# Attention: VectorE scales unit i-1's probabilities ahead of unit i's mask and maximum

## The reference

```python
def causal_block_attention(q, k, v, scale):
    outs = []
    for blk in range(S // Q_BLOCK):                 # 8 blocks of 128 queries
        q0 = blk * Q_BLOCK
        kend = q0 + Q_BLOCK
        s = jnp.einsum('bqhd,bkhd->bhqk', q[:, q0:kend], k[:, :kend]).astype(jnp.float32) * scale
        mask = jnp.arange(kend)[None, :] <= (q0 + jnp.arange(Q_BLOCK))[:, None]
        s = jnp.where(mask, s, jnp.float32(-1e30))
        prob = jax.nn.softmax(s, axis=-1).astype(v.dtype)
        outs.append(jnp.einsum('bhqk,bkhd->bqhd', prob, v[:, :kend]))
    return jnp.concatenate(outs, axis=1)
```

## Time and profile before

| | us |
|---|---|
| median of 3 runs (lowest to highest) | 3570.2 (3569.43 to 3573.05) |
| the profiled execution | 3566.13 |
| its span | 3564.8 |
| TensorE busy | 3452.5 |
| VectorE busy | 1780.7 |
| ScalarE busy | 1286.8 |

### The profile page before, as it was taken

How to read it: one execution, slowest core, us unless ns; L and a number is a source line. 1 busy time by engine, 2 the same in 40 slices (tenths; PEclk the granted TensorE clock), 3 DMA queues, 4 the chain that set the end, 5 groups by cost and what they waited for, 6 DMA issues and landing times.

```text
span 3564.8 us, 48555 instructions
## 1 busy us (share of the span) xinstructions
PE 3452.5 (97%) x20382; PEld 2809.8 (79%) x20382; DVE 1780.7 (50%) x2367; ACT 1286.8 (36%) x2193; POOL 1054.3 (30%) x592
## 2 busy tenths in 40 slices
PE   7999999999999999999999899999999999999999
PEld 6788888887678788888887677777787788888887
DVE  3665746437755433333335639975544444434444
ACT  4443433344433312222224547771232333223223
POOL 3212122110033233333331126662353223322221
PEclk9999999999999999999999999999999999999999
DMA  5101101110045211111112222223554311111111
GB/s 151 40 24 43 47 24 46 51 34 7 1 156 175 72 52 48 48 48 54 48 48 95 98 77 80 83 77 106 181 188 133 107 53 48 48 48 49 52 48 54
DMA packets 282377, 253.14 MB, mean 71 GB/s; under 512 B 11621, under 2 KB 221985, under 8 KB 282160
## 3 DMA queue, kind: packets, MB, share of 16 engines
q1 hardware_dynamic: 267552, 215.76, 19.9%
q10 hardware_dynamic: 11520, 25.17, 1.9%
q0 software_dynamic: 3088, 9.10, 0.7%
HBM read 213.29 MB, written 36.70 MB: 70 GB/s over the span
## 4 chain that ended last, share of the span: by engine, by line


## 5 line engine op out<-in xcount | busy, mean ns | idle before, releaser
L414 POOL TENSOR_TENSOR weight_lo<-stage,weight_hi 128x1024 fp32r<-128x1024 f32 (+4 forms) x265 | 624.1, 2360 | 1381.3 <-ACT weight_hi L406 1352.8
L377 PE MATMUL psum<-hT_hi,weight_hi 128*128 128x512 f32 x2240 | 885.2, 395 | 5.7 <-DVE hT_lo L563 5.7
L378 PE MATMUL psum<-hT_lo,weight_hi 128*128 128x512 f32 x2240 | 874.2, 390 | 0.0
L379 PE MATMUL psum<-hT_hi,weight_lo 128*128 128x512 f32 x2240 | 874.0, 390 | 0.0
L377 PEld LDWEIGHTS psum<-hT_hi,weight_hi 128*128 128x128 f32 x2240 | 422.2, 188 | 102.8 <-issue 7.5
L378 PEld LDWEIGHTS psum<-hT_lo,weight_hi 128*128 128x128 f32 x2240 | 422.3, 189 | 90.5 <-issue 4.3
L379 PEld LDWEIGHTS psum<-hT_hi,weight_lo 128*128 128x128 f32 x2240 | 421.9, 188 | 88.6
L406 ACT ACTIVATE weight_hi<-stage 128x1024 fp32r<-128x1024 f32 (+4 forms) x329 | 315.9, 975 | 478.3 <-PE psum L379 439.5
L2092 DVE TENSOR_TENSOR x<-x,psum 128x512 f32<-128x512 f32 x416 | 279.6, 686 | 219.0 <-PE psum L379 218.4
L377 PE MATMUL psum<-weight_hi,act_hi 128*128 128x512 f32 x864 | 339.0, 392 | 0.0
L379 PE MATMUL psum<-weight_hi,act_lo 128*128 128x512 f32 x864 | 338.7, 392 | 0.0
(11 more groups left out here) (379 smaller groups left out, 5261.5 us busy)
## 6 DMA issues: line engine op xcount, KB each, us to landing
stage<-in_w_in SPq DMA_DIRECT2D x64, 512.0 KB, 3.9
stage<-in_w_up SPq DMA_DIRECT2D x44, 512.0 KB, 3.9
scratch_gates<-gate ACTq DMA_DIRECT2D x64, 256.0 KB, 2.0
gs<-scratch_gates SPq DMA_DIRECT2D x64, 256.0 KB, 2.7
stage<-in_w_out SPq DMA_DIRECT2D x32, 512.0 KB, 4.9
stage<-in_w_ffn_up SPq DMA_DIRECT2D x32, 512.0 KB, 4.2
stage<-in_w_ffn_down SPq DMA_DIRECT2D x32, 512.0 KB, 3.7
stage<-in_w_down SPq DMA_DIRECT2D x22, 512.0 KB, 3.5
```

What stands on the lines that cost most here:

```text
L377: q.matmul(out, stat[0], mov[0], start=first, stop=False)
L378: q.matmul(out, stat[0], mov[1], start=False, stop=False)
L379: return q.matmul(out, stat[1], mov[0], start=False, stop=final)
L414: g.q.tensor_tensor(lo, K.staged(w), hi.bitcast(F32), ALU.subtract).then_inc(*S.w_lo_pool.up(w))
```

## The change

In each turn the step `scale_p` of unit i-1 moves from behind the first piece of feed to the very front, ahead of `score` of unit i. Only VectorE has a part in `scale_p`, so only VectorE's queue changes: reciprocal and scaling of i-1 now stand ahead of mask, maximum and negation of i.

```diff
     for i in range(len(UNITS) + TURN_LAG + OUT_LAG):
+        if 0 <= i - 1 < len(UNITS):
+            o.do("scale_p", i - 1)
         if i < len(UNITS):
             pair = UNITS[i][0]
...
         fed += 1
         more = 1 if fed > 0 else 0
         advance(feed, more)
-        if 0 <= i - 1 < len(UNITS):
-            o.do("scale_p", i - 1)
         if 0 <= i - TURN_LAG < len(UNITS):
             o.do("turn_p", i - TURN_LAG)
         advance(feed, more)
```

## The result

The changed kernel takes 3581.2 us in the median of 6 runs (3579.4 to 3585.2), the kernel before 3571.0 (3567.7 to 3573.1), run beside it. The ratio is 1.0028, with a 95% interval of 1.0018 to 1.0038: slower by some 10 us. The profiled execution of the changed kernel took 3582.0, its span 3580.7.

A forecast was written before the change was run, and what follows sets the result against it. It took TensorE, busy 97%, to bound the kernel, except where it waits for VectorE. 1.0 + 3.2 + 3.2 = 7.4, with half clock 8.6, on 3566.13 profiled gives 3574.7; the median, 4.1 higher, 3578.8, said as 3579; range 3571 to 3587.

The forecast's parts named there:

- the entry: Start of the last pair, which has no feed: its first mask (7h0) comes 2.7 us late.
- The closed loop: Attention without feed: exponential, scaling, maximum, next exponential run with nothing beside them, 2.80 us a unit, 44.7 per 16-unit pair.
- (a): Stretches where the next pair's projections are fed in and TensorE is full: the change costs nothing.
- (b): Start of attention: two kT copies queue behind the early scaling, so TensorE's third score comes 1.0 us later.
- (c): First two pair ends: outputs wait for VectorE's copy behind 7h0's maximum, 1.6 us at each, 3.2 together.
- (d): Last pair: enters 2.7 us late, plus 0.5 by the loop: 3.2, or 4.4 with TensorE's clock at half there.
- The clock: TensorE's granted clock may fall to half behind stalls; a slow stretch costs up to 1.5 us.
- a rival of chance 0.17: The clock falls in several new places, up to five in the last pair and at its end: 3586; chance 0.17.
- the likeliest case: The loop in attention as summed: 3579, own range 3573.6 to 3581; chance 0.55.
- The faster rival: Ahead of the stalls the mask loses nothing, TensorE's 13.1 us of waits for P go: 3557; chance 0.10.

The follow-up runs named there:

- the further operation: One more VectorE maximum per unit between maximum and negation, result unused: changed order 3598.8 against 3569.5 before, 1.0079; old order 3581.7, 1.0031.
- the first run above: Scaling ahead of the mask only in turns 1 to 47, the first three pairs, against the kernel before: 3575.3 against 3568.7, 1.0017.
- the later transposes in the old order: Kernel before with TURN_LAG 3 in place of 2, TensorE transposing the probabilities one turn later: 3567.4 against 3568.7, 0.9996.

## Why the prediction was right

The forecast was 3579.0, the median 3581.2, 10.2 us over before where 8 to 9 were forecast. The mechanism was the one named, and the terms of the sum can be read off. But that the sum came out so near is in part luck: its terms were 1.0 for the start, 3.2 for the two inner ends, 2.7 for the entry, 0.5 for the last pair and 1.2 for the clock there; the profile has 1.1, 0.8, 2.2, 2.8 (the clock in it) and, behind the last scaling, 2.4 that the sum didn't have. What the inner ends cost too little, the last pair and its tail cost too much.

- The closed loop. 2.80 us a unit were worked out from the trace before; the large masks of the changed kernel lie 5.61 us apart for two units. Shown by the trace, by the further operation, which is paid in full in the changed order, and by the run with the copy on ScalarE, where all of the last pair goes at 5.61.
- (a) Fed stretches cost nothing: the edit in these turns alone gives 0.9995. The cover has its limit: with 0.32 us more in each unit's chain the pairs with feed lost too.
- (b) The start, 1.0: the third score's wait grew from 3.06 to 4.09.
- (c) The inner ends, 1.6 each at full clock: 1.2. The step took all of it for the copy behind the maximum; the copy moved to ScalarE takes 0.6 away, and the other 0.6, by the waits, goes with the scores' bank, which the step did not name. The size was near for half of the reason.
- (d) The last pair, 0.5 by the loop: 2.8. The sum had 1.7 here with the 1.2 for the clock at the entry. It assumed that the loop alone sets the pace from the first unit on. The last ten units do keep to it; the first ones are slower, 6.97, 5.92 and 6.05 for two units instead of 5.61, since the masks there waited for scores behind slow or late outputs. By the profiles in which the clock stayed at 1.00 at the entry, 1.6 of this is the clock. Most of the rest, 0.5, goes with the copy on ScalarE: it is VectorE's copy, for which the outputs at 973.84 waited 1.74 us, and the step had looked for such a wait only at the pair ends. The entry, 2.7 late, was 2.2: the first mask came 4.8 later than before, 2.6 of which TensorE had already brought along.
- The clock. In the sum it had 1.2 at the entry (8.6 less 7.4); at the end it was a rival of chance 0.17, with up to five new places. It fell at the entry of the last pair, as before, and in one new place, the two waits for the last P. At the end of the first pair, where it had fallen before (57.65 us between the masks of 6h0 there, 56.00 a pair later), it did not, so that end came out 0.4 shorter than before instead of 1.2 longer. This is what the sum lacked at the end: last scaling to last output 7.1 us instead of 4.7. Keeping TensorE at work there took 3.5 us off by the profile and some 7 by the ratios, so the rival was part of the truth beside the likeliest case. It did not come as a rule of how long a wait is. In the changed kernel waits of 0.94, 1.74, 0.85, 1.40 and 0.88 us in the last pair left the clock at 1.00 from 969 to 1005, while it fell in the first run above behind one of 0.88. The rule that I weighed, of the Trainium skill, "TensorE: Matmul & The Clock Gate", section "A second HAM failure mode: psum-queue depth-cycling", that frequent short idles between groups of matmuls make the clock swing, the traces thus bear out in part: it does fall behind such waits, in some executions and some places, and not in most of them.
- The faster rival (13.1 us of stalls gone, 3557) was wrong on two counts. The stalls went, but others came; and the later transposes in the old order, which all but remove them, leave the time the same (0.9987 to 1.0005): 2.9 us came off the last pair, and the bank is late at nearly the same time elsewhere.

The first three pairs alone cost 6.6 us in the medians and 5.1 within attention in the profile. Against before these 5.1 are 1.1 at the start, 0.4 and 2.1 between the masks of 6h0 (58.06 and 58.07 against 57.65 and 56.00), 0.2 from there to the last scaling, and 1.3 behind it, where the list is that of before but the clock was at 0.64 from 1004 to 1008. So 0.8 at each inner end and the 1.3 of the tail are clock and not order. What one execution pays in such a place varies by 0.8 to 1.7 us with the clock, and a single profile is no measure of a difference of that size.

What stays open: what decides between the two levels behind a given wait; whether the second block's 3.9 us belong to the change; and whether the last 14 transposes brought more than the 3.5 us that the profile shows, for which the intervals are too wide.

## What to carry to other kernels

Before work is moved ahead on an engine because somebody waits for its result, look at what it must itself wait for, and at what then queues behind it: here a step that waited for ScalarE went ahead of the step for which ScalarE waited, and two overlapping halves became one loop. Add up that loop from the trace and compare it with the present pace stage by stage; where the pace is slower for another reason the move is free, and where it isn't the difference is paid. And a stall of so many us is worth no more than the distance to the next thing that is late, which only an experiment that removes it alone will tell.

## What was not expected of the hardware

- The same wait in the same place of the same list was followed by either level of the granted clock: 0.88 us ahead of the outputs at the first pair end by 1.00 in the changed kernel (834.72) and by 0.57 in the run of the first three pairs (836.06). In the kernel before, the wait of 1.73 us for P at a pair end was followed by 1.00 at 900.28 and, one pair on, by 0.50 at 957.
- Behind a wait of 1.24 us and then one of 1.98 it was at 0.50 to 0.52 from 1005 to 1017; with 14 transposes of no use in the second wait, of which 0.45 was left, it stayed at 1.00, and the kernel was faster, by 3.5 us in the profile. Work that computes nothing shortened the kernel.
- In the same way, 58 such transposes in four waits kept it at 1.00 through all of attention, where before it was 0.98 in the mean. Ahead of the third score this is more than the luck of one execution: all thirteen profiles without filling there have the clock under 1.00 between 788 and 800, and this one has not.
